# Router logits made tile by tile from the added rows, with column scales on the router and the row factor on the logits

## The reference

```python
x = x + mod_l[2] * y_l                       # y_l: merged branches @ w_out
h = rms_norm(x, norm2) * (1 + mod_l[4]) + mod_l[3]
aff = softmax(h @ w_router, axis=-1)         # 16 experts
top_w, top_idx = top_k(aff.transpose(0, 2, 1), cap)   # 64 latent, 32 context rows for each expert
# gather rows, SwiGLU experts, scatter back with top_w
```

## Time and profile before

| | |
|---|---|
| timed runs | 2642.32, 2653.34, 2653.73 us (median 2653.34) |
| profiled execution, its own time | 2644.56 us |
| its span in the profile | 2642.8 us |
| TensorE busy | 94% of the span |
| VectorE, ScalarE busy | 40%, 26% |
| mean granted TensorE clock | 0.989 |
| projection tail to experts, layer 0 | from about 774.5; adds end 848.75; experts from 906.6 |
| the same, layer 1 | adds end 2099.6; first gather of the experts from 2135.2 |

### The profile page before, as it was taken

How to read it: one execution, slowest core, us unless ns; L and a number is a source line. 1 busy time by engine, 2 the same in 40 slices (tenths; PEclk the granted TensorE clock), 3 DMA queues, 4 the chain that set the end, 5 groups by cost and what they waited for, 6 DMA issues and landing times. The chain is left out here.

```text
span 2642.8 us, 41041 instructions
## 1 busy us (share of the span) xinstructions
PE 2488.9 (94%) x17564; PEld 1566.6 (59%) x17564; DVE 1060.5 (40%) x2329; ACT 674.8 (26%) x1322; POOL 87.6 (3%) x145
## 2 busy tenths in 40 slices
PE   5999999999899899999999999998999999999998
PEld 3888877777687434443444478876676643343432
DVE  4545354344674313223232564545358431111113
ACT  3621232221543112111121363143236311010101
POOL 1000100000000000000100000100000000000000
PEclk9999999999999899999999999999999999999999
DMA  6111566255641689897989312232216379999996
GB/s 216 57 49 33 143 194 201 66 178 174 213 173 54 263 347 385 309 396 296 378 347 354 141 41 65 65 97 75 72 57 202 135 279 410 409 409 409 409 409 279
DMA packets 241828, 580.72 MB, mean 220 GB/s; under 512 B 11462, under 2 KB 120240, under 8 KB 240624
## 3 DMA queue, kind: packets, MB, share of 16 engines
q1 hardware_dynamic: 232160, 550.21, 56.1%
q0 software_dynamic: 9488, 27.90, 3.3%
HBM read 554.94 MB, written 23.13 MB: 219 GB/s over the span
## 5 line engine op out<-in xcount | busy, mean ns | idle before, releaser
L971 PE MATMUL ps<-h_hi,m_lo 128*128 128x512 f32 (+1 forms) x1152 | 344.3, 370 | 1.7 <-DVE arena L2147 1.7
L1395 PE MATMUL ps<-arena 128*32 128x512 f32 x1740 | 259.2, 593 | 1.6 <-ACT arena L1819 1.1
L1396 PE MATMUL ps<-arena 128*32 128x512 f32 x588 | 258.0, 593 | 0.0
L971 PEld LDWEIGHTS ps<-h_hi,m_lo 128*128 128x128 f32 x1152 | 207.0, 189 | 53.2 <-issue 16.8
L944 PE MATMUL ps<-m_lo,h_hi 128*128 128x256 f32 (+1 forms) x1248 | 233.2, 289 | 5.2 <-DVE m_lo L2120 2.9
L971 PE MATMUL ps<-h_lo,m_lo 128*128 128x512 f32 (+1 forms) x576 | 204.3, 355 | 0.0
L944 PEld LDWEIGHTS ps<-m_lo,h_hi 128*128 128x128 f32 x1248 | 196.1, 194 | 13.7 <-issue 9.7
L1541 PE MATMUL ps<-arena 128*64 128x512 f32 x832 | 187.8, 597 | 11.1 <-DMA arena<-in_moe_w_up 8.5
L944 PE MATMUL ps<-m_lo,h_lo 128*128 128x256 f32 (+1 forms) x624 | 177.3, 284 | 0.0
L1395 PEld LDWEIGHTS ps<-arena 128*32 128x32 f32 x1740 | 70.3, 110 | 164.2 <-issue 160.7
L944 PE MATMUL ps<-h_hi,m_lo 128*128 128x512 f32 (+1 forms) x512 | 141.7, 354 | 7.8 <-DVE h_lo L2225 6.9
(11 more groups left out here) (398 smaller groups left out, 4517.0 us busy)
## 6 DMA issues: line engine op xcount, KB each, us to landing
arena<-in_moe_w_up SPq DMA_DIRECT2D x101, 1024.0 KB, 12.9
arena<-in_moe_w_gate SPq DMA_DIRECT2D x100, 1024.0 KB, 11.7
arena<-in_moe_w_down SPq DMA_DIRECT2D x100, 1024.0 KB, 13.2
ring<-in_w_in SPq DMA_DIRECT2D x42, 1024.0 KB, 5.4
arena<-in_ada_w SPq DMA_DIRECT2D x40, 1024.0 KB, 5.4
oT<-in_moe_w_up SPq DMA_DIRECT2D x27, 1024.0 KB, 14.9
oT<-in_moe_w_down SPq DMA_DIRECT2D x24, 1024.0 KB, 9.1
oT<-in_moe_w_gate SPq DMA_DIRECT2D x16, 1024.0 KB, 9.4
```

The source lines that it names most:

```text
L971: last = mm(to, w[:, k, cols], h[:, k, seg], start=n == 0 and k == 0, stop=n == 2 and k == KD - 1)
L1395: mm(ps[r][32 * b:32 * b + 32, :], c_xg[:, k, j, 32 * b:32 * b + 32], w, start=k == 0, stop=k == KD - 1)
L1396: last = mm(ps[r][96:128, :], c_xg[:, k, j, 32 * r:32 * r + 32], up[:, kk, 512:1024], start=k == 0, stop=k == KD - 1)
```

## The change

Nothing is normed ahead of the router. The router is scaled by column once for each segment (`r_gain`), while the output projection runs, and the shift's share of the logits is summed into a bias row (`r_sum`, one product with ones inside the projection, `r_bias`). Behind the projection each tile of added rows `x_sb` is transposed (8 transposes into two banks), copied by ScalarE (half) and VectorE (half) into `xT`, and multiplied with the scaled router: 8 products whose weights are 128x128 blocks of `xT` and which stream 16 columns. VectorE writes the logits of a tile straight to `aff` as bank x row factor + bias. Two tiles are transposed ahead. The five fillers ahead of the router go; six fillers stand behind the last logits, ahead of the affinity transposes. `xn2` is still made for the experts, its last tile later in VectorE's order. The transposed logits `lgT`, their transposes and their sums are gone, and so is SyncE's wait for the logits in layer 0. TensorE no longer waits for the last add at the end of `merge`.

```diff
@@ TensorE, in place of norm_transposes(l)
+            def router_logits(l):
+                n, y0 = NQ[l], before("y_ok", l)
+                def turned(ti):
+                    t = q_tiles(l)[ti]
+                    first, second = ((ps[6], ps[7]), (ps[1], ps[2]))[ti % 2]
+                    pe.wait_ge(y_ok, max(y0 + n + ti + 1, bank_read(2) if ti % 2 else 0))
+                    if ti >= 2:
+                        pe.wait_ge(h_lat, before("h_lat", l) + ti - 1)
+                        pe.wait_ge(h_ctx, before("h_ctx", l) + ti - 1)
+                    for bank, up, ks in ((first, hl_up, range(4)), (second, hc_up, range(4, KD))):
+                        for k in ks:
+                            last = tr(bank[:, tile(k % 4)], x_sb[:, t, tile(k)], ident)
+                        last.then_inc(up, 1)
+                def logits(ti):
+                    pe.wait_ge(h_lat, before("h_lat", l) + ti + 1)
+                    pe.wait_ge(h_ctx, before("h_ctx", l) + ti + 1)
+                    if ti == 1:
+                        pe.wait_ge(y_ok, bank_read(3))
+                    if ti >= 2:
+                        pe.wait_ge(lgT_ok, before("lgT_ok", l) + 2 + ti - 1)
+                    s = 0 if q_tiles(l)[ti] >= CT else 1
+                    for k in range(KD):
+                        last = mm(ps[(0, 3)[ti % 2]][:, 0:E], xT[ti % 2][:, k, :], r_gain[:, s, k, :], start=k == 0, stop=k == KD - 1)
+                    last.then_inc(lg_up, 1)
+                turned(0)
+                turned(1)
+                for ti in range(n):
+                    logits(ti)
+                    if ti + 2 < n:
+                        turned(ti + 2)
+                kept_running(ps[5], 6)
@@ TensorE, merge(l), output projection
                         for n, k in enumerate(range(KD) if half else OUT_K):
+                            if (q, n) == (1, 4):
+                                pe.wait_ge(lgT_ok, before("lgT_ok", l) + 1)
+                                mm(ps[6][:, 0:NSEG[l] * E], ones, r_sum[...], start=True, stop=True).then_inc(lg_up, 1)
...
-                pe.wait_ge(y_ok, before("y_ok", l) + q)
                 pe.wait_ge(grow_ok, before("grow_ok", l) + 4 * NSEG[l])
@@ TensorE, route(l)
-                pe.wait_ge(lgT_ok, before("lgT_ok", l) + 1)
-                for t in q_tiles(l):
-                    bank, at = (ps[2], t - CT) if t >= CT else (ps[3], t)
-                    last = tr(bank[:, LG_ROWS * at:LG_ROWS * at + LG_ROWS], lgT[0:LG_ROWS, tile(t)], ident[0:LG_ROWS, 0:LG_ROWS])
-                last.then_inc(lg_up, 1)
                 pe.wait_ge(aff_ok, before("aff_ok", l) + 1)
@@ ScalarE, in place of modulate(l)
+            def turned_copied(l, ti):
+                if ti >= 2:
+                    act.wait_ge(lg_up, before("lg_up", l) + ti)
+                act.wait_ge(hl_up, before("hl_up", l) + KD + ti + 1)
+                do(xT[ti % 2][:, 0:4, :], ps[(6, 1)[ti % 2]][:, :], ACT.Copy).then_inc(h_lat, 1)
...
                 for ti in range(NQ[l]):
+                    if ti == NQ[l] - 1:
+                        turned_copied(l, 0)
                     act.wait_ge(y_ok, before("y_ok", l) + NQ[l] + ti + 1)
                     square(s2, ti, xn2)
...
+                turned_copied(l, 1)
                 rooted(s2, NQ[l] - 1)
-                modulate(l)
+                for ti in range(2, NQ[l]):
+                    turned_copied(l, ti)
@@ VectorE
+            def router_scaled(l):
+                dve.wait_ge(small_in, before("small_in", l) + 48)
+                for s in range(NSEG[l]):
+                    v.tensor_tensor(r_gain[:, s, :, :], router[:, 0:KD, :], scl[...], ALU.mult)
+                    last = v.tensor_tensor(r_shift[:, s, :, :], router[:, 0:KD, :], modT[l][...], ALU.mult)
+                link(last)
+                for s in range(NSEG[l]):
+                    last = v.tensor_reduce(r_sum[:, s, :], r_shift[...], AX_X, ALU.add)
+                last.then_inc(lgT_ok, 1)
+            def logits_kept(l, ti):
+                t = q_tiles(l)[ti]
+                dve.wait_ge(lg_up, before("lg_up", l) + 1 + ti + 1)
+                dve.wait_ge(lgT_ok, before("lgT_ok", l) + 2 + ti)
+                v.scalar_tensor_tensor(aff[:, t, :], ps[(0, 3)[ti % 2]][:, 0:E], st[:, 24 + t:25 + t], r_bias[...],
+                                       ALU.mult, ALU.add).then_inc(lgT_ok, 1)
+            def normed_and_routed(l):
+                s, n = 2 * l + 1, NQ[l]
+                turned_copied(l, 0)
+                scaled(s, n - 2)
+                turned_copied(l, 1)
+                mean(s, n - 1)
+                logits_kept(l, 0)
+                turned_copied(l, 2)
+                scaled(s, n - 1)
+                for ti in range(1, n):
+                    logits_kept(l, ti)
+                    if ti + 2 < n:
+                        turned_copied(l, ti + 2)
...
                 dve.wait_ge(m_ok, before("m_ok", l) + q)
+                router_scaled(l)
                 for n in range(2 * NSEG[l]):
                     diagonal(n)
...
-                normed_last(2 * l + 1)
-                modulate(l)
...
+                normed_and_routed(l)
...
+                if NSEG[l] > 1:
+                    link(v.memset(work[0:48, :], -1.0))
                 dve.wait_ge(aff_exp, before("aff_exp", l) + 1)
@@ SyncE, pair_loads(l, g)
                     if l == 0 and n == PAIR_SLOTS:
                         sp.wait_ge(xn2_out, 16 * NT)
-                        sp.wait_ge(lg_up, 1)
```

More of the change, by code:

```diff
@@ L294, in hybrid_kernel @@
                      for t in (m_hi[:, :, :].rearrange("p a b -> p (a b)"), oT_hi[:, :, :].rearrange("p a b -> p (a b)")[:, 8 * KB:24 * KB])]
-        work, chosen, slotT, lgT = carve(ar, 68, SEQ), carve(hTf, 9, SEQ), carve(hTf, 12, SEQ), carve(ar, 70, TOK)
+        work, chosen, slotT = carve(ar, 68, SEQ), carve(hTf, 9, SEQ), carve(hTf, 12, SEQ)
+        xT = [carve(hTf, 4 * i, KD, P) for i in range(2)]
+        r_gain, r_shift, r_sum, r_bias = carve(hTf, 18, 2, KD, E), carve(hTf, 19, 2, KD, E), carve(hTf, 20, 2, E), carve(hTf, 20.25, 2, E)
         ye_l, ye_c = carve(hTf, 6, 2, D), carve(hTf, 14, D)
@@ L568, in hybrid_kernel @@
         NORMS = [n for l in range(DEPTH) for n in (NT, NQ[l])] + [SEQ // P]
-        CTX_NORMS = [n for l in range(DEPTH) for n in (1, NSEG[l] - 1)]
         def col(row):
@@ L1008, in kept_running @@
                     mm(bank[:, :], ident, cst[:, 0:512], start=True, stop=True)
[L1010 to L1020, removed]
-                        for k in ks:
[L1022 to L1042, removed]
@@ L1328, in merge @@
                         for n, k in enumerate(range(KD) if half else OUT_K):
+                            if (q, n) == (1, 4):
+                                pe.wait_ge(lgT_ok, before("lgT_ok", l) + 1)
+                                mm(ps[6][:, 0:NSEG[l] * E], ones, r_sum[:, 0:NSEG[l], :].rearrange("p a b -> p (a b)"), start=True, stop=True
+                                   ).then_inc(lg_up, 1)
                             for row in gate_rows_beside(l, q, n):
@@ L1661, in _ @@
                 merge(l)
-                norm_transposes(l)
+                router_logits(l)
                 route(l)
@@ L1725, in scattered_rows_squared @@
                 rooted(s, NORMS[s] - 1)
[L1727 to L1732, removed]
+            def turned_copied(l, ti):
+                if ti >= 2:
+                    act.wait_ge(lg_up, before("lg_up", l) + ti)
+                act.wait_ge(hl_up, before("hl_up", l) + KD + ti + 1)
+                do(xT[ti % 2][:, 0:4, :].rearrange("p a b -> p (a b)"), ps[(6, 1)[ti % 2]][:, :], ACT.Copy).then_inc(h_lat, 1)
             def modulated_high(l):
@@ L1736, in modulated_high @@
                     for i, (up, seg, bank) in enumerate(((hl_up, LAT, ps[2 + k % 2]), (hc_up, CX, ps[4 + k % 2]))):
-                        act.wait_ge(up, KD * 2 * l + k + 1 if i == 0 else KD * sum(CTX_NORMS[:2 * l]) + k + 1)
+                        act.wait_ge(up, before("hl_up", l) + k + 1)
                         do(h_hi[:, k, seg], bank[:, 0:seg.stop - seg.start], ACT.Identity, scale=scl[:, 0, k, i:i + 1],
@@ L2206, in gains @@
                                               ALU.add, ALU.mult)
[L2208 to L2216, removed]
+            def router_scaled(l):
+                dve.wait_ge(small_in, before("small_in", l) + 48)
+                for s in range(NSEG[l]):
+                    v.tensor_tensor(r_gain[:, s, :, :], router[:, 0:KD, :], scl[:, 1, :, s].unsqueeze(2).to_broadcast([P, KD, E]), ALU.mult)
+                    last = v.tensor_tensor(r_shift[:, s, :, :], router[:, 0:KD, :], modT[l][:, 24:32, s].unsqueeze(2).to_broadcast([P, KD, E]), ALU.mult)
+                link(last)
+                for s in range(NSEG[l]):
+                    last = v.tensor_reduce(r_sum[:, s, :], r_shift[:, s, :, :].rearrange("p k e -> p e k"), AX_X, ALU.add)
+                last.then_inc(lgT_ok, 1)
```

(13 more changed lines are left out.)

12 lines of the change are left out of this document (8 added, 4 removed).

## The result

The changed kernel takes 2669.48 us (median of four, 2668.22 to 2670.51) beside 2653.53 us for the kernel before (2642.32 to 2653.82): ratio of the means 1.007, 95% interval 1.0043 to 1.0097 (the medians are 16 us apart, since three of the four runs before are near 2653.6 and one is 2642.32). Measured again beside 16 runs of the kernel before (2647.28), it took 2667.11: 1.0075, 1.0061 to 1.0089, that is some 20 us. It is slower, as forecast, and by a little less than the forecast amount (22.1 us).

What follows compares the result with a forecast made beforehand. TensorE, busy 94% of the span, was taken as the bound. 15.0 - 0.6 + 7.3 + 0.4 = +22.1 us on the profiled 2644.56 gave 2666.7; with the mean of all four, 2648.5, the forecast was 2671, range 2650 to 2685.

Steps and rivals of the forecast that it cites:

- The point to watch: In each layer, when the affinity transposes can start; a shift there was to pass on to the end.
- Weights set the pace: In the logit products, weight loads and not columns set the time: 1.8 us a tile at 2.4 GHz, 3.5 at 1.2.
- The clock falls after the first tile and stays down: Behind each projection, 1.2 GHz from the first tile's logits until the fillers; layer 0's logits end at 876.4.
- The fillers come last: Six fillers, 6.9 us in layer 0 to 883.3, delay the affinity transposes; the softmax would be ready at 878.8.
- What should cost nothing: Hidden work: VectorE's added products and sums, 1.5 us in layer 0, and SyncE's expert weights there starting about 4 us later.
- The bias product: Two passes on TensorE inside each projection, 0.2 us a layer, +0.4 us in all.
- the 0.6 us that I took off: Layer 0's affinity transposes run at full clock behind the fillers: -0.6 us.
- the two points: Start of the affinity transposes in both layers: +15.0 us in layer 0, +7.3 us in layer 1.
- (a): Rival: clock stays up behind both projections because transposes between the logits suffice; sum about 0, 2645 to 2649; chance 0.14.
- (b): Rival: at half clock only transposes stretch, weight loads do not; +9 us, 2653 to 2658; chance 0.04.
- (c): Rival: the six fillers do not bring the clock up and take 10.2 us; +29 us, 2677; chance 0.06.
- (d): Rival: (a), and slot products and layer 1's first gather find full clock; -5 us, 2640 to 2644; chance 0.02.

Runs made afterwards that it cites:

- e2: Changed kernel with each logit product streaming 128 columns instead of 16, router scaled for both segments in layer 1 too: 2643.42 us, ratio 0.9993 to the kernel before.
- b_no_lead: Kernel before the change without its five fillers ahead of the router's transposes: 2647.23 us beside 2647.28, ratio 1.0.
- e1: Changed kernel without the six fillers behind the last logits: 2655.12 us, ratio 1.0041 to the kernel before.
- e4: Changed kernel with the 128-column stream of e2 and no fillers behind the last logits: 2640.14 us, ratio 0.9973 to the kernel before.
- e3: Changed kernel with one more wide filler ahead of each tile's logits but the first: 2661.94 us, ratio 1.0068 to the kernel before; repeated unaltered, 1.0071.
- e6: Changed kernel with 64 columns streamed in each logit product instead of 16, router scaled as in e2: 2649.79 us, ratio 1.0008 to the kernel before.

## Why the prediction was right, step by step

**The point to watch, and that it passes on.** Right. Behind layer 1's affinity transposes the rest takes 26.9 and 499.4 us before and 26.9 and 499.3 after: the weight stream was moved as a whole. Layer 0's experts take 581.9 and 581.7.

**Weights set the pace.** Right: 16 passes, 1.78 us from start to start at full clock (850.67 to 852.45) and 3.27 at half (857.82 to 861.09 by the next transposes), where I had 1.8 and 3.47. The half-clock pass is 0.205 and not 0.217 us. Part of that was my working: I divided 4.34 us by all twenty passes, where at full clock I had taken off the last load's own time first; done alike (0.33 us for one load there) it is 0.211. This, with the next, is why layer 0 came out short.

**The clock falls after the first tile and stays down.** Right in kind in both layers. In layer 0 it fell at about 854.0 and not at 852.3, so that one tile's transposes and part of the next logits still ran at full speed: 1.5 us less than I charged. Layer 0's logits end at 874.5, forecast 876.4. In layer 1 they take 14.7 us from 2117.97 to 2132.66, forecast 15.6. What the prediction had for a reason, that narrow products let the clock fall, is what e2 tested and bore out.

**The fillers come last.** Right: 6.88 us (874.53 to 881.41) for 6.9 forecast in layer 0, 7.57 in layer 1; the affinities are ready at 876.88, forecast 878.8. Layer 0 moved by +12.9 (forecast +15.0), layer 1 by +7.1 (forecast +7.3). That layer 1 is so close is luck: its logits were 0.9 us shorter than forecast and its fillers 0.7 longer.

**What should cost nothing.** The router's scaling and sums on VectorE took from 778.40 to 779.89, and VectorE still idled 6.17 us behind the first diagonal, for 7.38 in the earlier trace rows:

```profile
778.40 0.28 DVE L2217 TENSOR_TENSOR hT<-router,scl 128x128 f32<-128x128 f32 x1
...
786.74 0.69 DVE L2769 TENSOR_TENSOR arena<-cst,modT 128x512 f32<-128x512 f32 x1 [6.17 <-PE ps L1358]
```

The bias product was put at 0.2 us a layer; the projections grew by 0.3 and 0.2. SyncE's first expert load in layer 0 is issued at 855.57, 1.4 us later than before and not the 4 that I wrote; it cost nothing. The affinity transposes run at full clock, 0.82 for 1.45 us, as said, but the 0.6 us that I took off for it did not reach the end: from their start to the first expert product it is 38.3 us in both kernels. The six slot transposes behind top-k took 0.60 us for 0.42 and the fillers behind the slot products 8.46 for 8.03, at a lower clock, and that used it up.

**The sum.** I had +22.1, of which 22.3 for the two points; they give +20.1 (12.93 and 7.14), and the timed ratios 19 to 20. The forecast of 2671 for 2669.48 is closer than the steps deserve: the 3.6 us of the stretch between, which I had no term for, made up for what layer 0 was short of in the first profile, and the baseline itself moved (2653.53, 2644.46, 2647.28 and 2646.71 for the same kernel in four series). What I can claim is the share, 0.83% forecast, 0.7% to 0.75% measured.

**The rivals.** (a), the clock stays up, is what e2 made happen: points 23.1 and 17.8 against 22.9 and 17.6 by (a)'s arithmetic (869.8 less 846.9, 2115.3 less 2097.7), and the total is then that of the kernel before. Its argument, that transposes alone keep the clock, did not carry over to transposes with narrow products between them. b_no_lead shows that it holds for transposes alone. (b), loads that do not stretch, is excluded by the 3.43 us rows. The sentence of the Trainium skill (TensorE: Matmul & The Clock Gate, Part 2, LDWEIGHTS) that a weight load takes its columns at 1.2 GHz agrees here at full clock (0.111 us a pass for 128 columns) and not at half (0.205), and the measurement decides. (c) did not occur: the clock was 1.00 from 878.0 on, 3.5 us into the fillers, which took 6.88 us and not 10.2. Nor did (d): the slot products ran at 0.50 again.

## What to carry to other kernels

Before turning a product round so that its small side is streamed, count loads: with 128x128 f32 weights a pass took about 0.11 us at full clock, whether 16, 64 or 128 columns went through. When 16-column passes fill a stretch, TensorE is busy all the time and may still be given 1.2 GHz, as here, where a pass then took 0.205 us. If the profile shows busy 100% and a granted clock of 0.50, widening what is streamed under the same loads can be free speed (here some 20 us for unused columns). Fillers belong where the engine waits anyway and no longer than it waits: six where the softmax leaves room for two cost 9 us in the changed kernel (e1) and about 5 with the clock up (e4).

## What the runs showed that I had not expected

One filler a tile held the clock in layer 0 and not in layer 1 (e3), and 64 columns likewise (e6): both are more fragile than streaming 128 columns, and e3's single runs spread over 21 us. Two profiles of the same kernel differ by up to 4.7 us of span with both routing points equal to 0.1 us, and the trace shows falls of the clock elsewhere that land differently; a difference of a few us between two single profiles means nothing until the stretch that holds it is known. And the five leading fillers of the kernel before, through which the clock stays at 1.00, buy nothing in the total (ratio 1.0, 0.9991 to 1.0009, without them):

```profile
847.20:853.20 6.00, 4.49 (x12) 1.96 (x11) 4.20 (x10) 1.45 (x4) 0.00 (x0) 1.00 0.61 245
```
